# Interleaving in the mixing stage of a hybrid decoder layer: a weight tile is broken at every fourth k instead of every second, with a new tile order

## The reference

```
n = rms_norm(h, ln_mix_pre)
da_q, da_k, da_v, dn_q, dn_k, dn_v, dn_z, dn_b, dn_a, ca_q, gate_logits = split(n @ w_in)
y_a = diff_attention(da_q, da_k, da_v, rel_bias, ...)            # 8 heads, causal, two softmax maps each
y_b = rms_norm(gated_delta_rule(conv(dn_q, dn_k, dn_v), g, beta)) * silu(dn_z)   # 8 heads
y_c = memory_attention(ca_q, split(rms_norm(mem) @ w_mem_kv))    # 4 heads, 256 memory tokens
mixed = sum_i sigmoid(gate_logits_i) * (y_i @ w_branch_i)
h = h + rms_norm(mixed @ w_out)
h = h + rms_norm(square(relu(rms_norm(h) @ w_ff1)) @ w_ff2)
```

## Time and profile before

| | |
|---|---|
| median of 3 runs | 1395.21 us (1392.79 to 1397.09) |
| profiled execution, its own time | 1393.79 us |
| span of its profile | 1392.0 us |
| mean granted TensorE clock | 0.991 |
| PE busy | 1366.7 us, 98% of the span |
| DVE, ACT, POOL busy | 774.4, 483.3, 199.7 us |
| matmuls and other instructions | 24486 in all, 10516 matmuls |
| moved by DMA | 143.14 MB, 103 GB/s in the mean |

### The profile page before, as it was taken

How to read it: one execution, slowest core, us unless ns; L and a number is a source line. 1 busy time by engine, 2 the same in 40 slices (tenths; PEclk the granted TensorE clock), 3 DMA queues, 4 the chain that set the end, 5 groups by cost and what they waited for, 6 DMA issues and landing times.

```text
span 1392.0 us, 24486 instructions
## 1 busy us (share of the span) xinstructions
PE 1366.7 (98%) x10516; PEld 1132.3 (81%) x10516; DVE 774.4 (56%) x1277; ACT 483.3 (35%) x778; POOL 199.7 (14%) x140
## 2 busy tenths in 40 slices
PE   8899999999999999999999999999899999999998
PEld 8689887887888888888788878888888888888886
DVE  6796227844765957679544634553455522355333
ACT  5354433433534435435344222112433212222231
POOL 1112000020000200002001322232322200022010
PEclk9999999999999999999999999999989999999998
DMA  5154322222222221232222466645213232223331
GB/s 212 61 174 140 107 69 91 84 70 70 68 71 89 92 70 60 64 106 69 86 77 92 152 211 184 194 137 183 75 47 106 91 100 97 92 91 92 90 91 60
DMA packets 46434, 143.14 MB, mean 103 GB/s; under 512 B 4944, under 2 KB 7416, under 8 KB 46328
## 3 DMA queue, kind: packets, MB, share of 16 engines
q1 hardware_dynamic: 46328, 141.59, 31.8%
HBM read 126.88 MB, written 16.27 MB: 103 GB/s over the span
## 4 chain that ended last, share of the span: by engine, by line
PE 91%; DVE 7%; ACT 1%; issue 1%; DMA 1%; SPq 0%; DVEq 0%; ACTq 0%
PE acc L1713 25%; PE acc L1715 24%; PE acc L1714 24%; PE ps_d L1867 2%; PE ps_a L1788 2%; PE ps_a L1799 1%; DVE w_lo L1296 1%; PE ps_d L1829 1%; DVE conv_y L1398 1%; PE ps_a L1778 1%; PE ps_a L1767 1%; PE ps_d L1839 1%; PE ps_d L1843 1%; PE ps_d L1845 1%; PE ps_a L1794 1%
## 5 line engine op out<-in xcount | busy, mean ns | idle before, releaser
L1713 PE MATMUL acc<-n_hi,w_hi 128*128 128x512 f32 (+1 forms) x984 | 395.6, 402 | 3.8 <-DVE n_lo L1586 2.4
L1715 PE MATMUL acc<-n_hi,w_lo 128*128 128x512 f32 (+1 forms) x984 | 382.2, 388 | 0.0
L1714 PE MATMUL acc<-n_lo,w_hi 128*128 128x512 f32 (+1 forms) x984 | 381.9, 388 | 0.0
L1296 DVE TENSOR_TENSOR w_lo<-w_raw,w_hi 128x1024 fp32r<-128x1024 f32 x200 | 284.6, 1430 | 147.8 <-ACT w_hi L998 147.0
L998 ACT CAST w_hi<-w_raw 128x1024 fp32r<-128x1024 f32 x200 | 209.6, 1049 | 437.8 <-PE acc L1715 437.6
L1713 PEld LDWEIGHTS acc<-n_hi,w_hi 128*128 128x128 f32 x984 | 186.7, 190 | 44.5 <-issue 5.1
L1715 PEld LDWEIGHTS acc<-n_hi,w_lo 128*128 128x128 f32 x984 | 186.5, 189 | 40.5
L1714 PEld LDWEIGHTS acc<-n_lo,w_hi 128*128 128x128 f32 x984 | 187.1, 190 | 35.1 <-issue 0.5
L1715 PE MATMUL acc<-h_hi,w_lo 128*128 128x512 f32 x256 | 101.0, 395 | 0.0
L1713 PE MATMUL acc<-h_hi,w_hi 128*128 128x512 f32 x256 | 101.0, 395 | 0.0
L1714 PE MATMUL acc<-h_lo,w_hi 128*128 128x512 f32 x256 | 101.0, 395 | 0.0
(11 more groups left out here) (336 smaller groups left out, 1933.1 us busy)
## 6 DMA issues: line engine op xcount, KB each, us to landing
w_raw<-weights SPq DMA_DIRECT2D x200, 512.0 KB, 3.6
gate_scratch<-gate_st SPq DMA_DIRECT2D x24, 256.0 KB, 2.9
g_in<-gate_scratch SPq DMA_DIRECT2D x24, 256.0 KB, 4.0
y_raw<-y_scratch SPq DMA_DIRECT2D x16, 256.0 KB, 3.7
x_tok<-x SPq DMA_DIRECT2D x4, 512.0 KB, 5.5
y_scratch<-y_st SPq DMA_DIRECT2D x4, 512.0 KB, 3.1
y_scratch<-d_ET SPq DMA_DIRECT2D x4, 512.0 KB, 3.8
y_scratch<-y_st SPq DMA_DIRECT2D x8, 256.0 KB, 2.4
```

The costliest lines, as they stand in the source:

```text
L1296: V_.tensor_tensor(w_lo[:, t % SPL], w_raw[:, t % RAW], w_hi[:, t % SPL].bitcast(F32), ALU.subtract).then_inc(lo_ready, 1)
L1713: mm(bank, wh, hi_of(k), start=start and k == 0, stop=False)
L1714: mm(bank, wh, lo_of(k), start=False, stop=False)
L1715: last = mm(bank, wl, hi_of(k), start=False, stop=stop and k == KT - 1)
```

## The change

A long tile of the mixing stage had four parts of two k and gets two parts of four k, as the short tiles had already. `ORDER` is another permutation of the same groups of tiles. In it the `mem` tiles come from tile 7 on instead of 9, and `z` 0 behind them; `conv` 1 comes one tile earlier; `head` 1 comes directly behind `head` 0 and ahead of `conv` 2; `z` 1 comes one tile earlier; 18 tiles instead of 16 follow `head` 7, and `z` 3 stands four gates behind it. `plan_order` itself, its durations and the rest of the kernel are the same.

```diff
--- before.py
+++ after.py
@@ -86,10 +86,10 @@
-ORDER = [("conv", 0), ("z", 0), ("gate", 1), ("mem", 0), ("cq", 0), ("gate", 1), ("cq", 1), ("conv", 1),
-         ("cq", 2), ("gate", 1), ("cq", 3), ("head", 0), ("conv", 2), ("head", 1), ("gate", 1), ("z", 1),
-         ("head", 2), ("gate", 1), ("head", 3), ("head", 4), ("conv", 3), ("gate", 1), ("z", 2), ("head", 5),
-         ("gate", 4), ("head", 6), ("head", 7), ("z", 3), ("gate", 14)]
+ORDER = [("conv", 0), ("gate", 1), ("mem", 0), ("z", 0), ("cq", 0), ("cq", 1), ("conv", 1), ("cq", 2),
+         ("gate", 1), ("cq", 3), ("head", 0), ("head", 1), ("conv", 2), ("gate", 1), ("z", 1), ("head", 2),
+         ("head", 3), ("gate", 1), ("head", 4), ("conv", 3), ("z", 2), ("gate", 2), ("head", 5), ("gate", 1),
+         ("head", 6), ("gate", 1), ("head", 7), ("gate", 4), ("z", 3), ("gate", 12)]
@@ -206,7 +206,7 @@
     spill = [i for i, s in enumerate(attn) if s[0] in ("cv", "ay")]
     short = lambda t: tiles[t][0] in ("mk", "mv")
     finished = lambda t: tiles[t][0] in ("dq", "dk", "dv", "dz")
-    parts = {t: ((0, 4), (4, 8)) if short(t) else ((0, 2), (2, 4), (4, 6), (6, 8)) for t in range(n_mix)}
+    parts = {t: ((0, 4), (4, 8)) if short(t) else ((0, 4), (4, 8)) for t in range(n_mix)}
     last = {t: ("PE", "main", t) + parts[t][-1] for t in range(n_mix)}
     busy, needs, queue = {}, {}, {}
```

## The result

The changed kernel takes 1401.37 us (median of 9 runs, 1399.5 to 1403.41), the kernel before 1392.95 us on the same chip (9 runs, 1390.65 to 1397.09). The ratio is 1.0055, 95% interval 1.0043 to 1.0068, some 6 to 9.5 us; the medians are 8.4 us apart. The time lies inside the predicted range, but the likeliest case (no change, 1397) did not come about. What did is one half of rival 2, a `y_lo` that comes late for tile 104, without the condition that rival 2 set for it (a last delta step behind tile 103).

What follows compares the result with a forecast made beforehand. The prediction took PE, busy 98%, as the bound. It summed 1393.8 + 0.5 (seams) + 1.5 (start) + 0 (end) = 1395.8, on the median's scale 1397 us; range for 8 in 10: 1390.5 to 1408.

Steps and rivals of the forecast that it cites:

- the likeliest case: Whole kernel: PE's work is conserved and both chains fit; 1391.5 to 1399.4 us, likeliest 1397, chance 0.52.
- rival 2: End of mixing stage: chains pass the last tile, delta step after tile 103, y_lo late; 1404 to 1414 us, chance 0.3.
- PE's work is conserved: Mixing stage and elsewhere: every matmul, split and DMA stays the same, only their order changes.
- merging saves nothing: Mixing stage: 24 of 129 breaks merge, each saving 0 give or take 0.05 us; +0.5 us taken.
- rival 4: Mixing stage: faster, since breaks cost; 24 at 0.2 us, perhaps with the waits, 1387.1 to 1390.4 us, chance 0.1.
- the start: Early mixing stage: short mem tiles come earlier and may wait for subtractions; net +1.5 us, between -3.3 and +4.3.
- Rival 3: Early mixing stage: slower by the start alone, both norms starve the short tiles in full; 1400.7 us, chance 0.08.
- the count of room: Mixing stage: gaps rounded up to four k put delta's end at tile 104.25 of 104, attention's at 101.
- my own mark: Stage's end: last delta step four or more tiles ahead of the first y_hi matmul would refute the count of room.
- I take the overrun as 0: End of mixing stage: chains cost nothing past the last tile, 0 us; up to one tile kept for the range.
- its own mark: Mixing stage: the prediction is wrong if waits there sum to over 5 us.
- Rival 1: Whole kernel: the forecast itself, work conserved and chains fitting; 1391.5 to 1399.4 us, chance 0.52.

Runs made afterwards that it cites:

- order with room: Changed kernel's four-k parts throughout, with another order of the same tile groups in which attention ends early; 1389.78 us, ratio 0.9980 to the kernel before.

## Why the prediction came out as it did

**Right: PE's work is conserved, and merging saves nothing.** Seams are dear: L1870 and L1783 back to back take 384.80 - 384.00 = 0.80 us after, where under 0.75 was to speak for rival 4.

```profile
384.00 0.60 PE L1870 MATMUL ps_d<-state,d_SCR 128*128 128x128 f32 x4
384.44 0.60 PE L1783 MATMUL ps_a<-cst,qkv_T 128*128 128x128 f32 x4
384.80 0.48 PE L1713 MATMUL acc<-n_hi,w_hi 128*128 128x512 f32 x1
```

Of 129 breaks 113 are left, not 105. The new order explains little of that: the old order with parts of four k has 110. A likely reason, not shown: moving each break to the next allowed place holds the other steps still, while in a chain a late step moves those behind it. The three kernels with 16, 17 and 21 fewer breaks (the changed one, fine parts from tile 72, order with room) have a stage that, less its waits, is 1.3 and 1.1 us longer and 0.8 shorter than before, the first two with 1.1 to 1.6 us of half clock in it: no gain that follows the breaks.

**Nearly right: the start.** I had +1.5 us net. The stage is 798.86 us long against 796.34, +2.5, of which 1.2 are more waiting (8.2 against 7.0 us between 22 and 818) and 1.1 by the comparison above the half clock behind the first wait. It wasn't w_lo for which the short tiles waited (0.3 us), but the evacuation of the gate tile ahead of them on ACT, which I had not looked at. Of the 3.3 us of waits that I counted as in reach, the 1.4 for conv_x is a wait of tile 6 for the evacuation of a `conv` tile that the change leaves in its place, and it is there in every run. PE's first main matmul came 0.9 us earlier in this execution, so that the stage ended only 1.6 later. Rival 3, both norms starving the short tiles, is refuted for the changed kernel; with the new order and fine parts the short tiles did wait 4.1 us for `w_lo`, but only half of it behind a norm.

**Half right: the count of room.** Attention was to end at tile 101 and ended at 100. The third pair began at tile 57 (57.75 was said), but its chain took 332 k to the last delta step, not 372: it ended at tile 98.5, over five tiles ahead of the first `y_hi` matmul, which by my own mark refutes the count of room for delta. Rounding every gap up is too harsh there; of 50 k added it took 10. For attention the same count was close: from the first head's v transpose, at tile 43.5, it took 452 k, where 456 were said.

**Wrong: "I take the overrun as 0".** The step measured both chains against the stage's end at tile 104. Attention must be done well before, since eight blocks still have to be loaded, cast and subtracted, 32.9 us, and the eighth is wanted 4.9 us into tile 104. So in the changed kernel the limit is 32.9 - 4.9 = 28 us, five long tiles, ahead of it: tile 99. The forecast of 101 was past it, and so was the real 100. As an estimate for other orders it is rough, since the same way took 23.8 to 39.7 us in the runs. The prediction had the row of the first `y_lo`, 14.0 us behind attention, but not the eighth's, 39.7 us behind it (814.06 - 774.33), and used neither for the forecast. Rival 2 named the wait for `y_lo`; it priced it by the delta chain's end (0.25 tile and the norm of O, 7 us, 1404), which never bound anything. The measured price is 5.2 us of waits. So it is partly luck that the time lies in the range: the range had been drawn up to 1408 for an overrun of the delta chain that did not happen. Seen as a change, the forecast was 2 us on a base of 1395.2, and the measured one 8.4 on 1392.95.

**Missing: the clock.** No term of the sum, and none of the rivals, had the half clock behind the gaps, 2.8 us, nearly a third of the loss. By its own mark, over 5 us of waits in the stage, the prediction would be wrong, with 8.2 us. But the mark was badly set: the kernel before has 7.0 us of them between 22 and 818 us, between 95 us and the first `y_hi` matmul it is 1.7 against 0.7, and what decided lay just behind that matmul, not ahead of it. (Rival 1's lower bound is off as well: 1395.2 - 4.2 is 1391.0, not 1391.5.)

**What stays open.** In the order with room, 3.1 us of the gain are found in the stage; the span of that one execution is 5.8 us shorter than before's, the median about 3. Of the rest 2.4 lie behind the stage, where both have the same waits, but the clock is 0.95 against 0.93 from 1000 to 1100 us and 0.99 against 0.98 behind; nothing shows that the order does that. That the half clock at 81 to 85 us costs 1.1 to 1.6 us rests on one execution against two. Whether `y_lo` could be had earlier from the same end of attention, with the loads of its blocks further ahead in SP's queue, was not tried, nor whether the order with room can be improved further.

## What to carry to other kernels

When an interleaved chain ends early, its spare time is not what lies between its last step and the end of the stage; subtract what its result still passes through, up to the last block (here a reload and split through two buffers, 33 us in the changed kernel and 24 to 40 in others, by what stands between the loads in SP's queue). Making the grain coarser cost nothing on the engine that is full, but it lengthens each dependent chain by the rounding, and an order tuned for one grain was not good for the other, in either direction (1402.7, 1411.7, 1397.8 us for the mixed pairs). A gap on TensorE can cost more than its length: 5.2 us of gaps drew 2.8 us of half clock here.

## What the runs showed of the hardware

- The granted clock fell to 0.50 behind three waits of 1.2, 0.9 and 3.1 us within 7 us and stayed there for six busy microseconds; it also fell behind a single wait of 1.8 us (79 to 81 us), to 0.50 from 83 to 85 us, in the executions of two kernels and not in those of two others whose instructions are the same up to there. PE is shown as busy all the while, so only the granted clock and the distances between starts tell it.
- A seam between two steps of small fp32 matmuls that write to different tiles (`ps_a`, `ps_d`) costs what a return to the main stream costs, 0.08 us. An fp32 matmul of 128 columns stands as two records in the trace and takes 0.20 to 0.22 us in a row of such (4 in 0.81, 28 in 6.2).
- A wait that the trace calls "issue" had a cause all the same: a bank of PSUM whose evacuation (80.44 to 81.03) stood behind two other operations in ACT's queue.
